# Where the first sample's key pages and the merge's up weights are loaded in a one-core decoder step

## The reference

```python
def fox_sample(q, k, v, logf, cache_k, cache_v, cache_logf, page_table):
    kp = cache_k[page_table].reshape(DB, past, H, Dh)      # 8 samples x 16 pages x 128 tokens
    vp = cache_v[page_table].reshape(DB, past, H, Dh)
    s_past = einsum('bqhd,bkhd->bhqk', q, kp) * scale + suffix + cn
    s_new  = einsum('bqhd,bkhd->bhqk', q, k) * scale + cn - cn'      # causal
    p = softmax(concat([s_past, s_new]))
    o = p[past part] @ vp + p[new part] @ v

def merge_branches(x, a_out, b_out, ga, gb, w_up_a, w_up_b, w_o):
    return x + (ga * (a_out @ w_up_a) + gb * (b_out @ w_up_b)) @ w_o

# the step: projections -> prompt attention and chunk MLP -> sample attention
#           -> merge_branches -> 32-expert MoE -> gated per-layer embedding -> final norm
```

## Time and profile before

| | before |
|---|---|
| median of 3 runs | 2118.53 us (2113.05 to 2121.91) |
| the profiled execution | 2117.44 us |
| its span, first to last instruction | 2115.8 us |
| PE busy | 1938.8 us (92%) |
| DVE, ACT, POOL busy | 602.7, 303.1, 187.2 us |
| mean granted TensorE clock | 0.953 of full speed |
| moved by DMA | 406.25 MB, mean 192 GB/s |

### The profile page before, as it was taken

How to read it: one execution, slowest core, us unless ns; L and a number is a source line. 1 busy time by engine, 2 the same in 40 slices (tenths; PEclk the granted TensorE clock), 3 DMA queues, 4 the chain that set the end, 5 groups by cost and what they waited for, 6 DMA issues and landing times. The chain is left out here.

```text
span 2115.8 us, 23169 instructions
## 1 busy us (share of the span) xinstructions
PE 1938.8 (92%) x8461; PEld 1026.4 (49%) x8461; DVE 602.7 (28%) x1405; ACT 303.1 (14%) x500; POOL 187.2 (9%) x290
## 2 busy tenths in 40 slices
PE   8999989799999966889799998789999999995897
PEld 4465445556566643555455554434444444441343
DVE  4201113333324333444232223501111011010686
ACT  1000001022223212333210000310000000000110
POOL 1000003200000010333100000100000000000220
PEclk9998999799999988999799998989999999998899
DMA  7020100351112028997611132559999999995331
GB/s 253 14 82 2 43 21 1 108 211 65 45 65 65 29 108 290 320 334 254 218 64 63 69 142 95 208 218 401 415 422 428 423 416 423 419 425 201 135 134 55
DMA packets 108816, 406.25 MB, mean 192 GB/s; under 512 B 18825, under 2 KB 36298, under 8 KB 96354
## 3 DMA queue, kind: packets, MB, share of 16 engines
q1 hardware_dynamic: 85138, 331.27, 40.6%
q0 software_dynamic: 16496, 56.15, 7.7%
q10 hardware_dynamic: 7072, 17.38, 2.1%
HBM read 354.48 MB, written 50.27 MB: 191 GB/s over the span
## 5 line engine op out<-in xcount | busy, mean ns | idle before, releaser
L1956 PE MATMUL psum<-arena 128*64 128x512 f32 (+1 forms) x1024 | 344.1, 599 | 1.4 <-DVE arena L2046 1.4
L789 PE MATMUL psum<-arena 128*128 128x363 f32 (+1 forms) x768 | 255.1, 477 | 9.9 <-DMA arena<-in_w_in 8.2
L1956 PEld LDWEIGHTS psum<-arena 128*64 128x64 f32 (+1 forms) x1024 | 130.1, 165 | 181.2 <-issue 179.4
L287 PE MATMUL psum<-arena 128*128 128x512 f32 x432 | 190.6, 601 | 0.0
L789 PEld LDWEIGHTS psum<-arena 128*128 128x128 f32 x768 | 140.2, 192 | 84.3 <-DMA arena<-in_w_in 8.5
L1993 PE MATMUL psum<-arena 128*64 128x512 f32 (+1 forms) x512 | 170.0, 595 | 1.0 <-DVE arena L2060 1.0
L287 PEld LDWEIGHTS psum<-arena 128*128 128x128 f32 x432 | 82.8, 194 | 100.7 <-issue 100.7
L2297 PE MATMUL psum<-arena 128*128 128x512 f32 x288 | 127.7, 602 | 1.6 <-DVE arena L2327 1.6
L1436 PE MATMUL psum<-arena 128*128 128x512 f32 x288 | 125.7, 594 | 1.6 <-PEq L1293 1.6
L1993 PEld LDWEIGHTS psum<-arena 128*64 128x64 f32 (+1 forms) x512 | 66.1, 163 | 101.9 <-issue 101.9
L1014 PE MATMUL psum<-ident,arena 128*128 128x128 f32 x512 | 70.8, 282 | 44.0 <-DMA arena<-in_cache_k 24.3
(11 more groups left out here) (267 smaller groups left out, 1942.3 us busy)
## 6 DMA issues: line engine op xcount, KB each, us to landing
arena<-in_w_exp_gate SPq DMA_DIRECT2D x32, 2048.0 KB, 13.9
arena<-in_w_exp_up SPq DMA_DIRECT2D x32, 2048.0 KB, 14.7
arena<-in_w_exp_down SPq DMA_DIRECT2D x32, 2048.0 KB, 10.9
arena<-in_cache_v POOLq DMA_DIRECT2D x128, 256.0 KB, 4.2
arena<-in_cache_k SPq DMA_DIRECT2D x128, 256.0 KB, 5.1
moe_out<-arena ACTq DMA_DIRECT2D x24, 512.0 KB, 11.9
arena<-in_w_in SPq DMA_DIRECT2D x5, 2048.0 KB, 19.9
moe_out<-arena SPq DMA_DIRECT2D x1, 9728.0 KB, 32.1
```

Of the source, the lines that this page charges most:

```text
L287: last = mm(c.bank[4 + r % 3][:, :], HT[:, k, t * P:(t + 1) * P], W[:, n + 1, k, :], start=(k == 0), stop=(k == KD - 1))
L789: done = mm(c.bank[7][:, 0:b - a], WG[:, blk % 2, k, q * P:(q + 1) * P], HT[:, k, a:b], start=(k == 0), stop=(k == KD - 1))
L1956: last = mm(out[rows_, :], XT[:, u % 2, k, rows_], c.ring_tile(LOAD[kind, u, r])[:, k, :], start=(k == 0), stop=(k == KD - 1))
```

## The change

The key buffer and the value buffer swap halves of the region: `KC` now lies where the prompt attention has `BH` and `WG`, `VC` in the lower half. Chunk 0 of `KC` is `BH[0]`, chunk 1 `BH[1]`, chunk 2 `WG[0]`, chunk 3 `WG[1]`. The page table is loaded at the start of the prompt attention's SP stream. The 16 key pages of sample 0 are issued from that stream: chunk 0 at piece 36, chunk 2 at piece 44, chunks 3 and 1 after the last piece's store. In the sample attention SP issues no key pages for sample 0, and the two up weights come behind the last key page of sample 7 instead of ahead of the first of sample 0. The numbers of the pages are now read by a helper: on SP four numbers and then four DMAs, on POOL all 16 numbers of a sample ahead of its first wait for `v_used`.

```diff
@@ stage_prompt_attention
+    cached_rows(c)
@@ SP
+            sp.dma_start(c.pages, c.page_table.rearrange("(o b) g -> o (b g)", o=1)).then_inc(c.pages_in, 16)
             sp.wait_ge(c.scan_out, 16)
...
+                if p == 36:
+                    sp.wait_ge(c.pages_in, 16)
+                    sp.wait_ge(ttr, 2 * parts_before(3 * NP))
+                    c.load_keys(sp, 0, 0)
+                if p == NPIECE - 4:
+                    sp.wait_ge(gate_mm, NPIECE - PER_BLOCK)
+                    c.load_keys(sp, 0, 2)
                 col, a, b = piece(p)
                 sp.wait_ge(gate_ev, p + 1)
                 sp.dma_start(c.gate_d[col, :, a:b], RAW[:, p % NRAW, 0:b - a]).then_inc(c.gate_out[p % NRAW], 16)
+            sp.wait_ge(gate_mm, NPIECE)
+            c.load_keys(sp, 0, 3)
+            sp.wait_ge(ttr, 2 * parts_before(N))
+            c.load_keys(sp, 0, 1)
             sp.wait_ge(c.blank_out, 16)
@@ new
+def cached_rows(c):
+    c.pages = view(c, T_AT + 864, DB * PAGES).bitcast(I32)[0:1]
+    c.KC = view(c, W_AT + NCH * CH * WA, NCH, CH, WA)
...
+    def page_numbers(eng, b, ch):
+        at = b * PAGES + ch * CH
+        return [eng.value_load(c.pages[0:1, at + g:at + g + 1], min_val=0, max_val=c.n_pool - 1) for g in range(CH)]
+
+    def load_keys(eng, b, ch):
+        numbers = page_numbers(eng, b, ch)
+        for g in range(CH):
+            eng.dma_start(c.KC[:, ch, g, :], c.cache_k[bass.ds(numbers[g] * P, P), :]).then_inc(c.k_in[ch], 16)
@@ stage_sample_attention
-    KC = view(c, W_AT, NCH, CH, WA)
-    VC = view(c, W_AT + NCH * CH * WA, NCH, CH, WA)
+    KC = c.KC
+    VC = view(c, W_AT, NCH, CH, WA)
@@ SP
-            sp.dma_start(pages, c.page_table.rearrange("(o b) g -> o (b g)", o=1)).then_inc(pages_in, 16)
...
-            sp.wait_ge(pages_in, 16)
             sp.wait_ge(c.sufd_out, 16 * H)
-            for n, w in enumerate((c.w_up_a, c.w_up_b)):
-                sp.dma_start(view(c, UP_AT + n * WBLK, KF, D), w).then_inc(c.up_in, 16)
             for b in range(DB):
                 if b >= 2:
                     sp.wait_ge(chunk_mm, NCH * (b - 1))
                 sp.dma_start(SUF[:, b % 2, :], c.sufd[:, b, :]).then_inc(bias_in[b % 2], 16)
+                if b == 0:
+                    continue
                 for ch in range(NCH):
-                    if b >= 1:
-                        sp.wait_ge(k_tr, U * (b - 1) + NPAIR * (ch + 1))
-                    for g in range(CH):
-                        at = b * PAGES + ch * CH + g
-                        page = sp.value_load(pages[0:1, at:at + 1], min_val=0, max_val=c.n_pool - 1)
-                        sp.dma_start(KC[:, ch, g, :], c.cache_k[bass.ds(page * P, P), :]).then_inc(k_in[ch], 16)
+                    sp.wait_ge(k_tr, U * (b - 1) + NPAIR * (ch + 1))
+                    c.load_keys(sp, b, ch)
+            for n, w in enumerate((c.w_up_a, c.w_up_b)):
+                sp.dma_start(view(c, UP_AT + n * WBLK, KF, D), w).then_inc(c.up_in, 16)
@@ POOL
-            pool.wait_ge(pages_in, 16)
+            pool.wait_ge(c.pages_in, 16)
             for b in range(DB):
+                numbers = [c.page_numbers(pool, b, ch) for ch in range(NCH)]
                 for ch in range(NCH):
                     if b >= 1:
                         pool.wait_ge(v_used, NCH * (b - 1) + ch + 1)
                     for g in range(CH):
-                        at = b * PAGES + ch * CH + g
-                        page = pool.value_load(pages[0:1, at:at + 1], min_val=0, max_val=c.n_pool - 1)
-                        pool.dma_start(VC[:, ch, g, :], c.cache_v[bass.ds(page * P, P), :]).then_inc(v_in[ch], 16)
+                        pool.dma_start(VC[:, ch, g, :], c.cache_v[bass.ds(numbers[ch][g] * P, P), :]
+                                       ).then_inc(v_in[ch], 16)
```

More of the change, by code:

```diff
@@ L917, in _ @@
                     keep_out(m - 2)
+CH = 4
+NCH = PAGES // CH
+def cached_rows(c):
+    c.pages = view(c, T_AT + 864, DB * PAGES).bitcast(I32)[0:1]
+    c.KC = view(c, W_AT + NCH * CH * WA, NCH, CH, WA)
+    c.pages_in = c.sem("pages_in")
+    c.k_in = [c.sem(f"k_in{i}") for i in range(NCH)]
+    def page_numbers(eng, b, ch):
[5 more added lines that the diff above has]
+            eng.dma_start(c.KC[:, ch, g, :], c.cache_k[bass.ds(numbers[g] * P, P), :]).then_inc(c.k_in[ch], 16)
+    c.page_numbers, c.load_keys = page_numbers, load_keys
 def stage_sample_attention(nc, c):
@@ L925, in stage_sample_attention @@
     AT8 = view(c, A_AT + NP * WA, NPAIR, P)
-    CH = 4
-    NCH = PAGES // CH
     U = NCH * NPAIR
     STRIP = 32
-    KC = view(c, W_AT, NCH, CH, WA)
-    VC = view(c, W_AT + NCH * CH * WA, NCH, CH, WA)
+    KC = c.KC
+    VC = view(c, W_AT, NCH, CH, WA)
     KTS = view(c, Q_AT, 2, NPAIR, CH * P)
@@ L943, in stage_sample_attention @@
     pace = view(c, t0 + 850, 2, NCH + 1)
-    pages = view(c, t0 + 864, DB * PAGES).bitcast(I32)[0:1]
     PTS = view(c, t0 + 1000, PAGES, P)
     c.up_in = c.kept_sem("up_in")
-    pages_in, cn_in = c.sem("pages_in"), c.sem("cn_in")
+    cn_in = c.sem("cn_in")
     bias_in = [c.sem(f"suffix_in{p}") for p in range(2)]
-    k_in, v_in = [c.sem(f"k_in{i}") for i in range(NCH)], [c.sem(f"v_in{i}") for i in range(NCH)]
+    k_in, v_in = c.k_in, [c.sem(f"v_in{i}") for i in range(NCH)]
     v_used, zeroed, blanked = c.sem("v_used"), c.sem("qb_zeroed"), c.sem("bias_zeroed")
```

## The result

| | before | changed |
|---|---|---|
| median | 2117.32 us (4 runs, 2113.05 to 2121.91) | 2096.15 us (4 runs, 2094.51 to 2097.85) |
| the profiled execution | 2117.44 us, span 2115.8 | 2094.77 us, span 2093.1 |

The ratio is 0.990 with a 95% interval of 0.9876 to 0.9924. The forecast was 2087.6 us: a gain of 31 us, of which 21 came. Of the two terms of the sum the head came as worked out and the tail came short (7.0 of 9.5 us); the rest was lost in smaller places.

A forecast was written before the change was run, and what follows sets the result against it. PE's idle time was taken as bound by transfers at the stage's head and by issuing at its tail. 2117.44 - 21.4 - 9.5 = 2086.5 us, plus 1.1 for the runs' median, gave 2087.6; own range 2083 to 2091, chance 0.62.

The forecast's parts named there:

- the head: Start of the sample attention: first transposes at 786.1 instead of 807.45, a gain of 21.4 us.
- the tail: Sample 7's products with the values: the last ends at 1018.6 instead of 1028.15, a gain of 9.5 us.
- the wide range: Whole kernel: 2082 to 2098 us, taking in the two partial cases and the bounds of the terms.
- the partial cases: Two rivals: POOL's issue no shorter, 2094 to 2097 us; head gives part back, 2091 to 2096; chance 0.14 each.
- Keys leave the head, minus 24.3; eight pages at the barrier, plus 2.9: Sample 0's key wait goes, minus 24.3 us; eight pages ending the prompt attention delay the barrier 2.9, bounds 0 to 13.
- Chunks at pieces 36 and 44 cost nothing: Prompt attention: chunks 0 and 2 each hold SP 4.4 us ahead of a gate store; cost 0, at most 8.8.
- Sample 1's pages, taken at 0 with an upper end of 3: Sample 1's keys land in time beside sample 0's values, SP's queue at 220 GB/s: cost 0, at most 3 us.
- Numbers ahead of the wait on POOL, minus 9.5: Tail, sample 7: value pages issued 0.66 us apart, all by 1012; gain 9.5 us, bounds 3.2 to 9.7.
- Up weights behind the last page, nothing: Up weights beside sample 6's values arrive before the merge: cost 0, cover 1 to 4 us, 4 us if values end late.
- Two of the signs: Against the forecast: L1014 (later L1044) waiting at 804 to 812; at the tail, L1070 (later L1100) still waiting for in_cache_v.
- the head gives part back: Rival: SP's issues stall before the barrier or sample 1's first chunks come late; 3 to 8 us less, 2091 to 2096; chance 0.14.
- The one on POOL's issue: Rival: value-page issue on POOL gets no shorter; only 21.4 us gained, 0 to 3 at the tail, 2094 to 2097; chance 0.14.

The follow-up runs named there:

- chunk1_early: The changed kernel with chunk 1 of sample 0's keys issued ahead of the last gate store instead of behind it: 2089.96 us, ratio 0.9871.
- ref: The changed kernel once more, with no edit, for a second trace: 2095.13 us, ratio 0.9896 to the kernel before.
- pagewise: The changed kernel, but POOL reads each page's number directly ahead of its DMA, as before: 2098.61 us, ratio 0.9915.
- hoist_only: The kernel before, with only POOL's 16 numbers of a sample read ahead of its first wait: 2111.84 us, ratio 0.9975.
- up_last: The kernel before, with only the two up weights moved behind the last key page of sample 7: 2106.58 us, ratio 0.9955.
- up_first: The changed kernel with the two up weights issued ahead of the loop over the samples again: 2098.43 us, ratio 0.9914.
- v0_early: The changed kernel with sample 0's value numbers read by POOL in the prompt attention, so those pages are issued earlier: 2089.79 us, ratio 0.9877.

## Why the prediction was right in kind and short in size

By the two profiled executions, the span shrank by 22.7 us instead of 30.9. Step by step:

- *Keys leave the head, minus 24.3; eight pages at the barrier, plus 2.9.* Right. From the last gate piece to the first transposes it is 22.1 us less against 21.4. From its last store to its last page SP took 9.2 us (8.9 forecast), and it ended 3.5 us behind PE. The barrier's price was avoidable: chunk1_early took all of it off.
- *Chunks at pieces 36 and 44 cost nothing.* Right: the prompt attention's waits are those of before, and ref reached its last gate piece at 767.9, ahead of the 768.8 of before.
- *Sample 1's pages, taken at 0 with an upper end of 3.* This is the first mis-sized term. The wait was 2.9 us, and the clock fell behind it, so that the stretch from the first transposes to sample 0's values took 3.7 us more (6.6 in ref). The step that failed is the share: I took 220 GB/s for SP beside POOL from a stretch in which SP's queue carried up weights. Those rows have 777 to 780 packets. These are of the same trace from 799 to 805 us, with keys and hardly any more up weights in SP's queue (columns as the earlier trace rows):

```profile
q0 software_dynamic: 387, 1.26, 64.6%
q1 hardware_dynamic: 386, 0.72, 38.4%
```

- *Numbers ahead of the wait on POOL, minus 9.5.* The mechanism was right and shown from both sides (pagewise, hoist_only), against the rule that the prediction cites, of the Trainium skill, "DMA: Bandwidth & Descriptors", section "Issuing engines are not separate DMA queues", that issue time is usually small beside the DMA itself. The size was 7.0 us. This is the second mis-sized term, and the step that failed is 16 pages at 0.66 us in one run. The pace was better, 0.59, but the hole of 2.6 us that I counted as gone stayed, and the last page is issued by 998.1, 12.9 us after PE let POOL go, not 10.6. It then lands only at 1003.7, as the queue moved 364 GB/s from 994 to 1002 (2.91 MB in 8 us): the rest of the tail is bound by transfers.
- *Up weights behind the last page, nothing.* Right in this trace but for 0.2 us, and as thin as said: in other traces PE waited up to 1.9 us. That they are out of the way at the head is worth more than I gave: up_last gains 11 us there by itself.
- *The rest.* 0.9 us inside the samples went with the stretch of low clock there. 1.2 us came ahead of the stage and did not repeat. 0.9 us lie behind the merge's start, where the low clock lasted 4.6 instead of 3.7 us; that explains about half of them, and the other half is open. 0.4 us were gained ahead of the merge. I had no term for any of them.

Two of the signs that I had named came: a wait of L1044 at 812 us and one for values at the tail. The forecast's own range, 2083 to 2091, was missed; the time lies in the wide range only because that takes in the partial cases. Of the rivals, "the head gives part back" (2091 to 2096) was nearest in kind. The one on POOL's issue (2094 to 2097) holds the measured time, but by luck: its mechanism fell with hoist_only. The head's 21.4 us alone would give 2097.1, as near, and hoist_only speaks against that in the same way.

## What to carry to other kernels

When a transfer is moved out of a stage's first wait, the order of the queue is worth reading first: here moving 4 MB behind the pages gave 11 of the head's 18 us before any buffer was swapped. For the share of two queues that are both busy, take a row in which both carry the transfers in question, and count packets as well as bytes. What an issuing engine does last in a stage stands in front of the barrier; one place earlier in its stream it can be free.

## What was unexpected

A 64 KB load behind 4 MB cost 8.6 us (up_first), and eight loads of 2 KB lost 3.0 us beside a burst of value pages (v0_early). A short wait can cost about twice its length: 3.0 us for keys was followed by 10 us at the 1.2 GHz level in ref, and from the first transposes to sample 0's values 6.6 us were lost. In the kernel before no stretch at that level lies between 811 and 1008 us. Every trace with the changed head but up_first's has one or two inside its samples, besides the one behind the wait for keys, each 3.4 us long and at a cost of 1.0 to 1.2 us. The changed head isn't needed for it, since hoist_only has one and up_last two. Each begins shortly behind a wait of 1.1 us for DVE, as in the rows under ref, but the same wait stands in other samples where the clock stays up. Why it falls is open.
